# Output projection and router of a hybrid decoder layer: tiles by quarters of the weights, router steps between products

## What is computed

```python
    merged = (jax.nn.sigmoid(g_a + b_gate[0]) * (y_attn @ w_attn_br)
              + jax.nn.sigmoid(g_s + b_gate[1]) * (y_ssd @ w_ssd_br))
    h = x + merged @ w_out
    hn = _rms_norm(h, norm2_w).reshape(b * L, D_MODEL)
    h = h + _hier_moe(hn, w_rc, b_rc, w_rf, b_rf, w_eg, w_eu, w_ed).reshape(b, L, D_MODEL)
```

## Time and profile before

| | |
|---|---|
| three timed runs | 2446.01 us (2440.57 to 2448.38) |
| profiled execution | 2425.19 us |
| its span, first to last instruction | 2422.9 us |
| `phase_out_router` in it, from VectorE's first to its last instruction | 1486.10 to 1670.99 us |
| first product, end of the last product | 1499.53, 1653.12 us |
| mean granted TensorE clock of the span | 0.896 |

### The profile page before, as it was taken

The page is one execution under the profiler, slowest core; times in us unless marked ns, Lnnn a source line. Parts: engine busy times, 40 slices in busy tenths (PEclk is TensorE's granted clock), DMA queues, the critical chain, the costliest instruction groups (busy, mean ns, idle before and its releaser), DMA issues. The chain is left out here.

```text
span 2422.9 us, 29824 instructions
## 1 busy us (share of the span) xinstructions
PE 1992.9 (82%) x11817; PEld 1769.1 (73%) x11817; DVE 1227.3 (51%) x1243; ACT 815.3 (34%) x1138; POOL 340.5 (14%) x360
## 2 busy tenths in 40 slices
PE   7999999599969998998822796994299999999950
PEld 7999999588869987887511696774178888888840
DVE  5244333156520204555338444222288888888845
ACT  4211111133312102221234110211177777777722
POOL 0000010445240002010210000000411111111004
PEclk9999999799978899999865898986599999999985
DMA  6355554443254435222162733224289999999937
GB/s 216 104 164 183 181 159 157 142 140 116 93 162 128 137 87 167 85 92 76 38 211 70 269 94 127 87 87 161 104 342 404 404 408 403 406 405 405 403 132 271
DMA packets 199752, 473.43 MB, mean 195 GB/s; under 512 B 31417, under 2 KB 153562, under 8 KB 186565
## 3 DMA queue, kind: packets, MB, share of 16 engines
q1 hardware_dynamic: 129956, 315.91, 36.0%
q0 software_dynamic: 17440, 76.82, 9.4%
q10 hardware_dynamic: 52224, 78.89, 9.1%
HBM read 376.65 MB, written 121.93 MB: 206 GB/s over the span
## 5 line engine op out<-in xcount | busy, mean ns | idle before, releaser
L2650 DVE TENSOR_TENSOR k_w_lo<-expert_raw,k_w_hi 128x4096 fp32r<-128x4096 f32 x96 | 424.1, 4420 | 113.5 <-ACT k_w_hi L2602 113.5
L2602 ACT CAST k_w_hi<-expert_raw 128x4096 fp32r<-128x4096 f32 x96 | 348.5, 3633 | 147.7 <-PE k_pu L74 59.3
L72 PE MATMUL a_acc<-a_w_hi,x_hi 128*128 128x256 f32 x648 | 186.3, 288 | 0.0
L73 PE MATMUL a_acc<-a_w_lo,x_hi 128*128 128x256 f32 x648 | 184.4, 284 | 0.0
L74 PE MATMUL a_acc<-a_w_hi,x_lo 128*128 128x256 f32 x648 | 184.4, 284 | 0.0
L72 PEld LDWEIGHTS a_acc<-a_w_hi,x_hi 128*128 128x128 f32 x648 | 125.6, 194 | 0.1
L73 PEld LDWEIGHTS a_acc<-a_w_lo,x_hi 128*128 128x128 f32 x648 | 125.5, 194 | 0.0
L74 PEld LDWEIGHTS a_acc<-a_w_hi,x_lo 128*128 128x128 f32 x648 | 125.3, 193 | 0.0
L937 PE MATMUL d_z_acc<-d_z_w_hi,x_hi 128*128 128x256 f32 x288 | 93.1, 323 | 22.1 <-DVE d_z_w_lo L923 21.0
L72 PE MATMUL k_po<-k_w_hi,k_h_hi 128*128 128x512 f32 x256 | 102.3, 400 | 10.6 <-DVE k_h_lo L2671 10.6
L72 PE MATMUL k_pg<-k_w_hi,k_x_hi 128*128 128x512 f32 x256 | 102.4, 400 | 5.2 <-DVE k_x_lo L2655 5.2
(11 more groups left out here) (424 smaller groups left out, 4918.1 us busy)
## 6 DMA issues: line engine op xcount, KB each, us to landing
expert_raw<-in_w_expert_gate SPq DMA_DIRECT2D x32, 2048.0 KB, 10.1
expert_raw<-in_w_expert_up SPq DMA_DIRECT2D x32, 2048.0 KB, 11.9
expert_raw<-in_w_expert_down SPq DMA_DIRECT2D x32, 2048.0 KB, 11.2
scratch_o_moe<-k_out ACTq DMA_DIRECT2D x32, 512.0 KB, 11.4
a_w<-in_w_in SPq DMA_DIRECT2D x15, 1024.0 KB, 7.1
scratch_u_tm<-h ACTq DMA_DIRECT2D x81, 128.0 KB, 2.2
h_sig<-scratch_gate_cm SPq DMA_DIRECT2D x8, 1152.0 KB, 5.5
scratch_o_moe<-h_zeros POOLq DMA_DIRECT2D x2, 4096.0 KB, 26.1
```

The lines of the kernel that those rows point to most:

```text
L72: nc.tensor.matmul(out, one_pass(a_hi), one_pass(b_hi), start=(i == 0), stop=False)
L73: nc.tensor.matmul(out, one_pass(a_hi), one_pass(b_lo), start=False, stop=False)
L2602: nc.scalar.copy(one_pass(w_hi[:, kind, :]), raw[:, c % NRAW, :]).then_inc(s_hi, 1)
L2650: nc.vector.tensor_tensor(one_pass(w_lo[:, kind, :]), raw[:, c % NRAW, :], w_hi[:, kind, :], ALU.subtract).then_inc(s_lo, 1)
```

## The change

`phase_out_router` is rewritten; nothing else is touched.

- The first three tiles (`FIRST`) are done quarter by quarter: for each quarter of `w_out`, once it is split, 24 matmuls of 256 columns for tile 0, 1 and 2. Tiles 3 to 8 keep two outputs of 512 columns.
- `m_hi` and `m_lo` have three buffers instead of two; a tile's buffer is free when its products are done (`s_mm`), and TensorE's drain and `s_mfree` are gone.
- The high parts of the weights are written by ScalarE (`high_wo`), VectorE makes the low parts (`low_wo`). Drains of VectorE after its last operations are gone; the increments hang on the operations.
- The router's steps are cut into `turn(n, half)`, four transposes, and `logits(n)`, and stand after half products, up to three tiles later than before.
- On VectorE the logits are taken (`take_logits`) two tiles behind the residual. On ScalarE the loop is unrolled and `squares(n)` and `take_turned(n)` are separate steps in an order written out.
- SyncE loads the first tile of `x` after two quarters, and the constants after the last quarter. The START increments are gone.

```diff
@@ -2168,143 +2168,219 @@
...
-        NR = 36
+        NR, NQ, QCOL, FIRST = 36, 4, D // 4, 3
         ident, eps, w2, br = sb("ident", [128, 128]), sb("eps", [128, 1]), sb("w2", [128, D]), sb("br", [128, NR])
-        wo, wr = sb("wo", [128, 2, KT, 256]), sb("wr", [128, KT, NR])
+        wo, wr = sb("wo", [128, 2, KT, QCOL]), sb("wr", [128, KT, NR])
         wo_hi, wo_lo = sb("wo_hi", [128, KT, D]), sb("wo_lo", [128, KT, D])
-        m_hi, m_lo = sb("m_hi", [128, KT, 2, 128]), sb("m_lo", [128, KT, 2, 128])
+        m_hi, m_lo = sb("m_hi", [128, KT, 3, 128]), sb("m_lo", [128, KT, 3, 128])
...
         p_h = ctx.enter_context(nc.psum_tensor("i_ph", [128, 3, 2, 512], f32))
...
-        s_wsplit, s_m, s_mfree = sm("wsplit"), sm("m"), sm("mfree")
...
-        for s in (*s_st, *s_hn_st, s_te, s_le):
-            nc.sync.sem_inc(s, START)
+
...
         with nc.Block() as block:
             @block.sync
             def _(sp):
                 def load_wo(q):
-                    sp.dma_start(wo[:, q % 2, :, :], T["w_out"][0].rearrange("(k p) n -> p k n", p=128)[:, :, 256 * q:256 * q + 256]
+                    if q >= 2:
+                        sp.wait_ge(s_wsplit, q - 1)
+                    sp.dma_start(wo[:, q % 2, :, :], T["w_out"][0].rearrange("(k p) n -> p k n", p=128)[:, :, quarter(q)]
                                  ).then_inc(s_wo[q % 2], 16)
+
+                def load_x(n):
+                    u = n % 3
+                    if n >= 3:
+                        sp.wait_ge(s_st[u], n // 3 * 16)
+                        sp.wait_ge(s_n, n - 2)
+                    sp.dma_start(x[:, u, :], T["x_all"][tile(n), :]).then_inc(s_x[u], 16)
+
                 load_wo(0)
                 load_wo(1)
+                load_x(0)
+                for q in (2, 3):
+                    load_wo(q)
+                load_x(1)
+                load_x(2)
+                sp.dma_start(w2[:, :], T["norm2_w"].broadcast_to([128, D])).then_inc(s_const, 16)
                 sp.dma_start(ident[:, :], T["ident"]).then_inc(s_const, 16)
-                sp.dma_start(w2[:, :], T["norm2_w"].broadcast_to([128, D])).then_inc(s_const, 16)
                 sp.dma_start(br[:, :], T["b_router"].broadcast_to([128, NR])).then_inc(s_const, 16)
                 sp.dma_start(wr[:, :, :], T["w_router"][0].rearrange("(k p) n -> p k n", p=128)).then_inc(s_const, 16)
...
+                for n in range(3, TILES):
+                    load_x(n)
 
             @block.vector
             def _(dve):
                 nc.vector.memset(eps[:, :], EPS).then_inc(s_eps, 1)
-                dve.sem_inc(s_xfree, 3)
 
                 def split_m(t):
-
-                    if t >= 2:
-                        dve.wait_ge(s_mfree, t - 1)
-                    split(nc, dve, T["m_T"][:, :, t * 128:(t + 1) * 128], m_hi[:, :, t % 2, :], m_lo[:, :, t % 2, :])
-                    dve.sem_inc(s_m, 1)
-                split_m(0)
-                for q in range(4):
-                    cols = slice(256 * q, 256 * q + 256)
-                    dve.wait_ge(s_wo[q % 2], (q // 2 + 1) * 16)
-                    split(nc, dve, wo[:, q % 2, :, :], wo_hi[:, :, cols], wo_lo[:, :, cols])
-                    dve.sem_inc(s_wsplit, 1)
-                split_m(1)
-                dve.wait_ge(s_const, 64)
-                for n in range(TILES):
-                    u, j = n % 3, n // 3
-                    dve.wait_ge(s_x[u], (j + 1) * 16)
+                    if t >= 3:
+                        dve.wait_ge(s_mm, t - 2)
+                    hi, lo = m_hi[:, :, t % 3, :], m_lo[:, :, t % 3, :]
+                    nc.vector.tensor_copy(one_pass(hi), T["m_T"][:, :, tile(t)])
+                    dve.drain()
+                    nc.vector.tensor_tensor(one_pass(lo), T["m_T"][:, :, tile(t)], hi, ALU.subtract).then_inc(s_m, 1)
+
+                def low_wo(q):
+                    dve.wait_ge(s_whi, q + 1)
+                    nc.vector.tensor_tensor(one_pass(wo_lo[:, :, quarter(q)]), wo[:, q % 2, :, :], wo_hi[:, :, quarter(q)],
+                                            ALU.subtract).then_inc(s_wsplit, 1)
+
+                def residual(n):
+                    u = n % 3
+                    dve.wait_ge(s_x[u], (n // 3 + 1) * 16)
                     dve.wait_ge(s_mm, n + 1)
                     nc.vector.tensor_tensor(x[:, u, :], x[:, u, :], p_h[:, u, :, :].rearrange("p a c -> p (a c)"), ALU.add
                                             ).then_inc(s_h, 1)
-                    if n + 2 < TILES:
-                        split_m(n + 2)
+
+                def normalised(n):
+                    u = n % 3
                     dve.wait_ge(s_rms, n + 1)
                     nc.vector.reciprocal(ms[:, u, 1:2], ms[:, u, 1:2])
                     dve.drain()
-                    dve.wait_ge(s_hn_st[u], j * 16 + START)
+                    if n >= 3:
+                        dve.wait_ge(s_hn_st[u], n // 3 * 16)
+                        dve.wait_ge(s_t, 2 * (n - 2))
                     nc.vector.scalar_tensor_tensor(hn[:, u, :], x[:, u, :], ms[:, u, 1:2], w2[:, :], ALU.mult, ALU.mult
                                                    ).then_inc(s_n, 1)
-                    dve.drain()
-                    dve.sem_inc(s_xfree, 1)
+
+                def take_logits(n):
                     dve.wait_ge(s_l, n + 1)
-                    nc.vector.tensor_tensor(T["logits"][:, n, 0:NR], p_l[:, 0:NR], br[:, :], ALU.add)
-                    dve.drain()
-                    dve.sem_inc(s_le, 1)
+                    nc.vector.tensor_tensor(T["logits"][:, n, 0:NR], p_l[:, 0:NR], br[:, :], ALU.add).then_inc(s_le, 1)
+
+                split_m(0)
+                low_wo(0)
+                split_m(1)
+                split_m(2)
+                for q in range(1, NQ):
+                    low_wo(q)
+                dve.wait_ge(s_const, 64)
+                for n in range(TILES):
+                    residual(n)
+                    if n + 3 < TILES:
+                        split_m(n + 3)
+                    if n >= 7:
+                        take_logits(n - 2)
+                    normalised(n)
+                    if 2 <= n < 7:
+                        take_logits(n - 2)
+                take_logits(TILES - 2)
+                take_logits(TILES - 1)
 
             @block.scalar
             def _(act):
+                def high_wo(q):
+                    act.wait_ge(s_wo[q % 2], (q // 2 + 1) * 16)
+                    nc.scalar.copy(one_pass(wo_hi[:, :, quarter(q)]), wo[:, q % 2, :, :]).then_inc(s_whi, 1)
+
+                def squares(n):
+                    u = n % 3
+                    act.wait_ge(s_h, n + 1)
+                    act.dma_start(T["h"][tile(n), :], x[:, u, :]).then_inc(s_st[u], 16)
+                    nc.scalar.activation(junk[:, :], x[:, u, :], ACT.Square, accum_out=ms[:, u, 0:1])
+                    act.drain()
+                    nc.scalar.activation(ms[:, u, 1:2], ms[:, u, 0:1], ACT.Sqrt, bias=eps[:, :], scale=1.0 / D)
+                    act.drain()
+                    act.sem_inc(s_rms, 1)
+
+                def take_turned(n):
+                    u = n % 3
+                    act.wait_ge(s_n, n + 1)
+                    act.dma_start(T["hn"][tile(n), :], hn[:, u, :]).then_inc(s_hn_st[u], 16)
+                    for half in range(2):
+                        act.wait_ge(s_t, 2 * n + half + 1)
+                        nc.scalar.copy(hnT[:, 4 * half:4 * half + 4, :], p_t[:, :, :]).then_inc(s_te, 1)
+
+                for q in range(NQ):
+                    high_wo(q)
                 act.wait_ge(s_eps, 1)
...
+                for n in range(FIRST):
+                    squares(n)
+                for t in range(FIRST, TILES):
+                    for n in ((0,), (1,), (2, 3), (4,), (5, 6), (7,))[t - FIRST]:
+                        take_turned(n)
+                    squares(t)
+                take_turned(TILES - 1)
                 for u in range(3):
-                    act.wait_ge(s_st[u], START + 48)
-                    act.wait_ge(s_hn_st[u], START + 48)
+                    act.wait_ge(s_st[u], 48)
+                    act.wait_ge(s_hn_st[u], 48)
 
             @block.tensor
             def _(pe):
...
+                def out_product(t, cols, out):
+                    return product(nc, out, [((m_hi[:, k, t % 3, :], m_lo[:, k, t % 3, :]), (wo_hi[:, k, cols], wo_lo[:, k, cols]))
+                                             for k in range(KT)])
+
+                def turn(n, half):
+                    if half == 0:
+                        pe.wait_ge(s_n, n + 1)
+                    if 2 * n + half >= 1:
+                        pe.wait_ge(s_te, 2 * n + half)
+                    for k in range(4):
+                        c = (4 * half + k) * 128
+                        last = nc.tensor.transpose(p_t[:, k, :], hn[:, n % 3, c:c + 128], ident[:, :])
+                    last.then_inc(s_t, 1)
+
+                def logits(n):
+                    pe.wait_ge(s_te, 2 * n + 2)
```

(85 more changed lines are left out.)

21 lines of the change are left out of this document (removed).

## The result

| | before | after |
|---|---|---|
| timed runs, median | 2443.29 us (2436.04 to 2448.38, four) | 2404.69 us (2401.5 to 2415.81, four) |
| ratio | | 0.9852, 95% interval 0.981 to 0.9894 |
| profiled execution, its span | 2425.19, 2422.9 | 2405.67, 2403.5 |
| the phase, VectorE's first instruction to the last logits' end | 184.9 | 151.4 |
| all the rest of that span | 2238.0 | 2252.1 |

The timed runs moved by 38.6 us (26 to 46 by the interval), the spans of the profiled executions by 19.4, the phase by 33.5. The forecast was 22.9. The last product ends here, as in the earlier trace rows, where its slot ends and the next matmul could start.

The account below looks back on a forecast made before the run. TensorE, busy 82% of the span, was taken as the bound. Its work placed anew gave -18.9 us to the last product and -4.0 in the tail, so 2446.0 - 22.9 = 2423.1 us, range 2411 to 2436.

Parts of the forecast that it names:

- The count of falls: Up to the last product, TensorE's clock falls four times at 1.85 us, 7.4 us; bounds one and seven.
- the chain: Tile 5: TensorE idles 4.3 us, from logits(1) through take_logits(1), residual(4) and squares(4) to ScalarE's copy for the turn.
- the clock holds: Work between products is mostly short, so only the 4.3 us wait brings a fall: about 2416; chance 0.20.
- The carry to the timed runs: The timed median lies 20.8 us above the profiled execution before; the same difference was added to the forecast.
- first product, from the phase's start: Start of the phase: one quarter of the weights suffices, so the first product comes 3.7 us earlier, at 1495.8.
- quarters with the slow start: First three tiles: 288 products of 256 columns at 0.119 us, 34.2 us, plus 2.3 for the start at 1.2 GHz.
- six tiles of products and the joins to the steps: Remaining six tiles: products of 11.0 us each, 66.0, and eleven joins between product and router steps at 0.2, 2.2.
- fourteen groups of transposes: Router steps before the last product ends: four transposes cost about 0.5 us where other work follows, 7.0 in all.
- seven groups of logits: Router steps before the last product ends: seven logit groups of 1.8 us, 12.6 in all.
- three waits within `both`: both(3), both(5) and both(6) lack a half product to hide ScalarE's copy: 0.8 us each, 2.4.
- tail: Last product to the phase's end: 13.9 us against 17.9, with squares(8) behind tile 7's copies and a slow clock.
- The rivals on the slow side: Falls at nearly every logit half, 2431 (0.15); hardly any gain, 2439 (0.06); many ordering waits in tiles 4-8, 2462 (0.04).

Follow-up runs that it names:

- after_again: The changed kernel run once more, unchanged: 2409.39 us, ratio 0.9844 to the kernel before; phase 154.4 us.
- spread_only: The change's spread router steps with the start of the kernel before: ratio 0.9897, phase 159.1 us.
- unchained: The change with VectorE's residual(4) and the split behind it ahead of take_logits(1), likewise for tiles 3 to 6: 2406.81 us, ratio 0.9845, phase 146.0 us.
- dve_high: The change with both parts of the weights made by VectorE again, as before: phase 151.3 us.
- warm_start: The change with 16 unread matmuls of 512 columns until the first weights are ready: phase 152.2 us.
- tail_order: unchained with both(7) moved ahead of the last half product, behind logits(6): phase 151.2 us.
- tail_filled: tail_order with unread matmuls of 256 columns where TensorE waits after the last product: phase 147.5 us.
- best: The change with unchained's order, both weight parts by VectorE, warm_start's 16 matmuls and tail_filled's tail: 2402.76 us, ratio 0.9846, phase 142.9 us.
- start_only: The change's quarters and ScalarE high parts, but router steps in one piece after each product, without the drain: ratio 0.997, phase 178.2 us.
- start_filled: start_only with four unread matmuls of 256 columns after each group of four transposes: phase 170.5 us.

## Why the prediction missed

The direction, the place and the mechanism came out, the size did not: 2423.1 forecast, with 2411 as the lower end, and 2404.69 measured. Two steps failed.

**The count of falls.** "its second half and both of tile 7 about 4 us, near the 4.86 that brought a fall six times of seven, so likely; ... I count four falls at 1.85: 7.4". The first trace has one fall, worth 1.3 us (0.9 in the products, 0.4 in the transposes): 6.1 too much. The second has two, worth 4.5. The pieces were 3.4 us long, not 4, and I treated them like 4.86. Over all traces: behind pieces of 3.4 us the clock fell 5 times of 34 (after, after_again, spread_only, unchained, dve_high, warm_start, tail_order, tail_filled, best), behind pieces of 4.4 to 4.9 us (at the full clock) 17 of 19 (before twice, start_only), behind the 7 us of the chain 5 of 5. (These are not independent draws: start_only's five follow each other at the same 17.0 us.) The rival "the clock holds" had the first trace right, and came nearest with 2416; I gave it 0.20. The Trainium skill's rule that I set beside it ("TensorE: Matmul & The Clock Gate", section "Why this matters for your kernels") doesn't settle it. TensorE never idled more than 0.68 us at once in start_only's five pieces of 4.4 us either, and there the clock fell every time. So one long idle stretch is not what these falls go with; what else it is stays open, as said at start_filled.

**The carry to the timed runs.** "The timed runs lie 20.8 us above it in the median; I carry that over". I took the difference between one profiled execution and the runs as fixed. It was chance: that execution had the shortest rest of thirteen, and none of the 35 timed runs of before in this study was as short (2425.88 to 2455.51). The profile after lies 1 us above its median instead. A forecast of 33.5 us from the same anchor would have given 2412.5, inside the range but with no room below; my range held no term for an execution's own scatter of 20 us in code that isn't touched. The 38.6 measured exceed the 30.5 to 33.5 of the phase by 5 to 8, and the interval contains both. With all the timed runs of this study the surplus shrinks: the 35 of before average 2442.3 and the eight of the change 2406.3, so 36.0, plus or minus 6, for a phase 32.1 shorter in the mean of its two traces. The six of best give 41.5 for 42.2, the ten of start_only 6.1 for 6.8. So no run shows that anything beyond the phase moved.

The terms of the sum, predicted and measured in the first trace:

| | predicted | measured |
|---|---|---|
| first product, from the phase's start | 9.7 | 9.4 |
| quarters with the slow start | 36.5 | 36.9 |
| six tiles of products and the joins to the steps | 68.2 | 66.7 |
| fourteen groups of transposes | 7.0 | 5.2 |
| seven groups of logits | 12.6 | 11.9 |
| three waits within `both` | 2.4 | 2.8 |
| the chain of tile 5 | 4.3 | 4.2 |
| falls of the clock | 7.4 | 1.3 |
| tail | 13.9 | 13.0 |

So besides the clock, the differences are small: four transposes between products cost 0.37 us instead of 0.5, and without the drain a join costs next to nothing, 0.1 us where I had taken 0.2 (bounds 0.05 and 0.42). Halving the columns of the first tiles cost what the earlier trace rows said: the last quarter's products start 0.12 us apart, as forecast from there. The 109 ns that I had set beside it from the Trainium skill ("TensorE: Matmul & The Clock Gate", section "Back-to-back issue gap") was too low for this stream. The chain of waits, found by following each engine's order, was right to 0.1 us by the count of the sum, in which the 3.91 us of the trace are 4.2, and unchained showed it by removing it. The first transfer came 0.86 us earlier against VectorE's memset, where 0.7 was taken for the START increments; no run takes out these increments alone. The rivals on the slow side did not occur: the chain was met once, and the quarters had no gap.

## What to carry to other kernels

Where TensorE's products are interrupted by small work that others must finish, cut that work into pieces and put each behind half a product: the waits vanish, and above all the clock stays up. Six falls at 1.85 us stood in the kernel before, so 11 us, where the weights by quarters gave 6.7 in start_only. When steps are respread over in-order engines, follow for each wait what stands ahead of the releasing instruction on its own engine; one early `take_logits` cost 4.6 and 6.2 us in the two traces. And don't anchor a forecast on one profiled execution: compare the part that is touched, and give the untouched rest its own scatter.

## What the hardware showed

- The same 1657 matmuls of the attention of the samples took 236.4 us in one execution and 254.5 in another of the same kernel, at a granted clock of 0.86 and 0.80.
- Eight unused matmuls of 256 columns in a tile's router steps made the tile 1.6 us shorter (17.02 to 15.43), as the clock went from 0.90 to 1.00; 16 ahead of the first product saved 1.4 to 2.6 us, 32 in the tail 2.4.
- ScalarE's cast of 128x2048 to the one-pass format took 1.90 us where VectorE's took 1.23; moving work to the idle engine lengthened the path that counted.
- A drain and an increment behind a tile's products cost TensorE 0.4 us: 0.42 us from the last product's slot to the first transpose in the earlier trace rows, none in start_only.
